# Expert tiles of a large and of a small expert in alternation, with single buffers for each kind

## The reference

```python
def swiglu(xb, wg, wu, wd):
    return (jax.nn.silu(xb @ wg) * (xb @ wu)) @ wd

# hier_moe, cut: 4 groups of 8 experts, top 2, D_MODEL 1024, D_EXPERT 512
def expert_block(args):
    xb, e = args
    return swiglu(xb, lp['w_eg'][e], lp['w_eu'][e], lp['w_ed'][e])
yb = lax.map(expert_block, (xin, block_e)).reshape(n_rows, d)
return jax.ops.segment_sum(yb[dest] * sw[:, None].astype(h.dtype), st, num_segments=t)
```

## Time and profile before

| | us |
|---|---|
| median of 3 runs | 2587.0 |
| lowest and highest | 2582.14 and 2589.04 |
| the profiled execution | 2590.32 |
| span of its instructions | 2589.0 |

### The profile page before, as it was taken

One profiled execution on the slowest core, in us unless ns is written; L12 is line 12 of the kernel. 1 busy time (PEld: TensorE's weight loads), 2 busy tenths in 40 slices (PEclk: granted clock), 3 DMA queues, 4 the chain that ended last, 5 costly groups with the idle time before them and its releaser, 6 DMA issues.

```text
span 2589.0 us, 31253 instructions
## 1 busy us (share of the span) xinstructions
PE 2462.0 (95%) x12362; PEld 1884.7 (73%) x12362; DVE 1414.8 (55%) x2034; ACT 1044.5 (40%) x1570; POOL 288.6 (11%) x256
## 2 busy tenths in 40 slices
PE   6999999999999989888999889999999999999999
PEld 4867768687777766655666577888888777788887
DVE  3575776778547665544445655434444577543442
ACT  2424343343445345554445554223243446422221
POOL 0010211112223201111111010000013000100000
PEclk9999999999999979999999989999999999999999
DMA  7324243432445269999999923232232111323322
GB/s 267 110 73 163 78 162 111 142 97 97 165 160 195 72 233 377 375 381 369 381 386 386 373 99 114 75 112 93 74 125 76 48 50 49 106 83 97 106 78 77
DMA packets 143400, 428.18 MB, mean 165 GB/s; under 512 B 19394, under 2 KB 33986, under 8 KB 142096
## 3 DMA queue, kind: packets, MB, share of 16 engines
q1 hardware_dynamic: 119136, 377.43, 41.1%
q10 hardware_dynamic: 12960, 25.19, 2.7%
q0 software_dynamic: 11152, 23.49, 2.6%
HBM read 411.62 MB, written 31.72 MB: 171 GB/s over the span
## 4 chain that ended last, share of the span: by engine, by line
PE 76%; DVE 9%; DMA 8%; ACT 4%; issue 2%; POOL 1%; SPq 0%; ACTq 0%; POOLq 0%; DVEq 0%
PE bank L666 18%; PE bank L667 18%; PE bank L668 18%; DMA more<-in_ed 4%; DVE HLB L326 3%; PE bank L1216 2%; PE bank L1218 2%; PE bank L1217 2%; DMA raw<-in_ed 2%; PE bank L1273 2%; ACT HLB L315 2%; PE bank L1573 1%; PE bank L1234 1%; PE bank L953 1%; PE bank L1596 1%
## 5 line engine op out<-in xcount | busy, mean ns | idle before, releaser
L326 DVE TENSOR_TENSOR HLB<-raw,HLB 128x1024 fp32r<-128x1024 f32 (+1 forms) x374 | 454.1, 1220 | 475.3 <-ACT HLB L315 471.0
L666 PE MATMUL bank<-HTh,HLB 128*128 128x512 f32 (+1 forms) x1358 | 548.5, 404 | 12.3 <-DVE HLB L326 7.5
L315 ACT ACTIVATE HLB<-raw 128x1024 fp32r<-128x1024 f32 x382 | 381.5, 1007 | 386.9 <-PE bank L668 277.6
L667 PE MATMUL bank<-HTl,HLB 128*128 128x512 f32 (+1 forms) x1358 | 534.0, 393 | 0.0
L668 PE MATMUL bank<-HTh,HLB 128*128 128x512 f32 (+1 forms) x1358 | 533.4, 393 | 0.0
L666 PEld LDWEIGHTS bank<-HTh,HLB 128*128 128x128 f32 x1358 | 257.4, 190 | 99.1 <-issue 27.3
L668 PEld LDWEIGHTS bank<-HTh,HLB 128*128 128x128 f32 x1358 | 257.6, 190 | 59.7
L667 PEld LDWEIGHTS bank<-HTl,HLB 128*128 128x128 f32 x1358 | 257.8, 190 | 56.7 <-issue 1.9
L326 DVE TENSOR_TENSOR HLB<-more,HLB 128x1024 fp32r<-128x1024 f32 x116 | 139.8, 1223 | 71.6 <-ACT HLB L315 68.5
L315 ACT ACTIVATE HLB<-more 128x1024 fp32r<-128x1024 f32 x116 | 121.7, 1062 | 79.3 <-DMA more<-in_ed 66.8
L666 PE MATMUL bank<-FAh,HLB 128*128 128x512 f32 x352 | 139.1, 395 | 0.0
(11 more groups left out here) (601 smaller groups left out, 4256.6 us busy)
## 6 DMA issues: line engine op xcount, KB each, us to landing
raw<-in_f SPq DMA_DIRECT2D x120, 512.0 KB
more<-in_eg SPq DMA_DIRECT2D x77, 512.0 KB
more<-in_ed SPq DMA_DIRECT2D x73, 512.0 KB
raw<-in_eu SPq DMA_DIRECT2D x65, 512.0 KB
more<-in_eu SPq DMA_DIRECT2D x63, 512.0 KB
raw<-in_ed SPq DMA_DIRECT2D x55, 512.0 KB
raw<-in_eg SPq DMA_DIRECT2D x51, 512.0 KB
raw<-in_wada SPq DMA_DIRECT2D x40, 512.0 KB
```

The costliest lines, as they stand in the source:

```text
L315: self.nc.scalar.activation(hi, raw, ACT.Copy).then_inc(*self.w_hi.next(n))
L326: self.nc.vector.tensor_tensor(lo, raw, hi.bitcast(F32), ALU.subtract).then_inc(*self.w_lo.next(n))
L666: mm(bank, ah, bh, start=(start and i == 0), stop=False)
L667: mm(bank, ah, bl, start=False, stop=False)
```

## The change

The diff replaces the list of blocks by two lists: `heavy`, the large experts 0 to 16, and `few`, for each step the small expert that goes with it (none in step 0, 17 to 31 in steps 1 to 15, none in step 16). A step has 12 places m. At places 0 to 7 TensorE takes one gate/up tile of the large expert and then one of the small; at 8 to 11 one down tile of the previous step's large expert and one of its small one. Between places 7 and 8 it turns in the next step's tokens of both; after place 11 it transposes both gated products. In step 16 the down tiles of small expert 31 stand at places 2 to 5. The loads follow the same order.

Each kind has single tiles of its own: `XG`, `XGh`, `XGl`, `YO`, `GT`, `GTh`, `GTl` for the large, `XQ`, `XL`, `GQ`, `GTL`, `YQ` for the small. A new use waits for the end of the former one. The room goes into `more`, which has 6 buffers (`NSLOT`) instead of 5. In this stage splits are planned up to 8 tiles ahead (`AHEAD_MIXED`) instead of 4. GpSimd gathers for step s + 2 once the tokens of step s + 1 are turned in. The part of the output that stays on chip (`kept`) is large expert 16's as before. `in_order` is as before, and so is the number of tiles, matmuls, transposes and splits.

```diff
+NSLOT = 6
+AHEAD_MIXED = 8
+WEAVE = 1
@@ Plan, "lend"
-                self.slots_now = NRAW + NMORE * (len(self.backs) + 1)
-                self.raw_free += [(NRAW + NMORE * len(self.backs) + i, None) for i in range(NMORE)]
+                mixed = len(self.backs) == 1
+                self.ahead = AHEAD_MIXED if mixed else AHEAD
+                lent = range(NRAW + NMORE, NRAW + NMORE + NSLOT) if mixed else range(NRAW, NRAW + NMORE)
+                self.slots_now = lent[-1] + 1
+                self.raw_free += [(i, None) for i in lent]
@@ Plan.advance
-        while self.split < min(len(self.slot), self.at + AHEAD):
+        while self.split < min(len(self.slot), self.at + self.ahead):
@@ pe_experts
+        def few_at(few, s):
+            return 8 if few[s] is not None else 2
...
+            turn_in(heavy[0])
+            for s, b in enumerate(heavy):
+                for m0 in range(0, 12, WEAVE):
+                    for m in range(m0, m0 + WEAVE):
+                        if m < 8:
+                            first(b, "eg" if m < 4 else "eu", m % 4)
+                        elif s:
+                            last(heavy[s - 1], m - 8)
+                    for m in range(m0, m0 + WEAVE):
+                        if few[s] is not None and m < 8:
+                            first_few(few[s], "eg" if m < 4 else "eu", m % 4)
+                        if s and few[s - 1] is not None and 0 <= m - few_at(few, s) < 4:
+                            last_few(few[s - 1], m - few_at(few, s))
+                    if m0 + WEAVE == 8 and s + 1 < len(heavy):
+                        turn_in(heavy[s + 1])
+                        if few[s + 1] is not None:
+                            turn_in_few(few[s + 1])
+                middle(b)
+                if few[s] is not None:
+                    middle_few(few[s])
+            for k in range(4):
+                last(heavy[-1], k)
@@ act_experts
+            def turn_in(s):
+                b = heavy[s]
+                for q in range(2):
+                    act.wait_ge(*S.pe_out.when(("xg", b, q)))
+                    if s:
+                        act.wait_ge(*S.pe_out.when(("eu", heavy[s - 1], 3)))
+                    activation(XGh[:, 4 * q:4 * q + 4, :], ...
@@ pool_experts
+            def gather(s):
+                b = heavy[s]
+                if s:
+                    pool.wait_ge(*S.pe_out.when(("xg", heavy[s - 1], 1)))
...
+            for s in range(len(heavy)):
+                if s + 2 < len(heavy):
+                    gather(s + 2)
+                    if few[s + 2] is not None:
+                        gather_few(s + 2)
+                if s and few[s - 1] is not None and few[s] is None:
+                    scatter_few(few[s - 1])
+                if s:
+                    scatter(heavy[s - 1])
+                if s and few[s - 1] is not None and few[s] is not None:
+                    scatter_few(few[s - 1])
@@ the order
-        blocks = list(range(STATIC))
-        for n in range(LIGHT):
-            blocks += [HEAVY + n, STATIC + n]
+        heavy = list(range(HEAVY))
+        few = [None] + list(range(HEAVY, 32)) + [None]
```

More of the change, by code:

```diff
@@ L500, in build @@
         phase(W1)
[L501 to L512, removed]
+        XG = here("XG", [128, 1024])
+        XQ = here("XQ", [128, 512])
+        XGh = here("XGh", [128, 8, 128], FR)
+        XGl = here("XGl", [128, 8, 128], FR)
+        YO = here("YO", [128, 1024])
         XL = here("XL", [128, 4, 128])
-        phase(W1 + 7680)
+        GQ = here("GQ", [128, 256])
         GTL = here("GTL", [128, 2, 128])
+        YQ = here("YQ", [128, 512])
         phase(W1)
         YI = here("YI", [128, 4, 2, 1024])
-        assert cur[0] == EARLY_YI
+        GT = here("GT", [128, 512])
+        GTh = here("GTh", [128, 4, 128], FR)
+        GTl = here("GTl", [128, 4, 128], FR)
+        more = here("more", [128, NSLOT, 1024])
         phase(W1)
@@ L654, in build @@
                        [raw[:, i, :] for i in range(NRAW)] + [early[:, i, :] for i in range(NMORE)]
-                       + [more[:, i, :] for i in range(NMORE)], HLB, counted.get("tiles", []),
+                       + [more[:, i, :] for i in range(NSLOT)], HLB, counted.get("tiles", []),
                        w_load + w_early + w_more, w_hi, w_lo, pe_out)
@@ L2067, in act_experts, with out_few @@
-            last(len(blocks) - 1)
+                    activation(YO[:, cols(4 * n, 4)], psum[("yo", b, n)][:, :], ACT.Copy, scale=weight).then_inc(
+                        *S.act_out.next(("yo", b, n)))
+            def out_few(s):
+                b = few[s]
+                column = NBLK + b - HEAVY
+                act.wait_ge(*S.pe_out.when(("yo", b, 3)))
+                act.wait_ge(*dve_out.when("wrow"))
+                if few[s - 1] is not None:
+                    act.wait_ge(*S.scattered.when(few[s - 1]))
+                activation(YQ[:, :], psum[("yo", b, 0)][:, :], ACT.Copy, scale=WROW[:, column:column + 1]).then_inc(
+                    *S.act_out.next(("yo", b, 0)))
@@ L2069, in act_combine @@
+            for k in range(4):
+                ring.hi(act, "ed", heavy[-1], k)
+            out(len(heavy) - 1)
         def act_combine():
@@ L2961, in dve_combine @@
+            for k in range(4):
+                ring.lo(dve, "ed", heavy[-1], k)
+            if S.kept:
+                keep(heavy[-1])
         def dve_combine():
@@ L3560, in build @@
                     e.wait_ge(*s.when("experts"))
-                e.wait_ge(*scattered.when(30))
+                e.wait_ge(*scattered.when("all"))
             found = {}
```

518 lines of the change are left out of this document (267 added, 251 removed).

## The result

The kernel after takes 2593.0 us (median of 17 runs, 2589.6 to 2599.2) where the kernel before takes 2584.7 on the same chip (17 runs, 2582.1 to 2590.2). The ratio is 1.0029, 95% interval 1.0022 to 1.0036: slower by 0.3%, where 2564 us and faster were forecast. The profiled execution took 2597.2 us (span 2595.9), 6.9 more than that of before.

The account below looks back on a forecast made before the run. TensorE and the DMA, both nearly full and starving in turns, were taken as the bound. A stage 24.1 us shorter, less 1 us at its end, took the median from 2587.0 to a forecast 2564 us, range 2548 to 2583.

Parts of the forecast that it names:

- the work added: TensorE in the expert stage: 180 round trips of matmul shape against 30, 180 x 0.20 = 36.0 us, ends 25 and 49.
- the pot: TensorE's 50.8 us of idle time in the expert stage, to fall to under 15.
- the sum: Expert stage: TensorE's 524.4 us plus waits and cover, 536.5 us instead of 560.6; 24.1 gained, 23.1 after the end's charge.
- Priced at nothing beyond the sum: Six extra buffers and splits eight tiles ahead: no time of their own; the gated load becomes the sixth instead of fifth.
- the hole: DMA dip at 1186 to 1190 us, where SyncE's load waits for a large tile's buffer; worth 2.1 us.
- shallow queue* rival: Large-tile buffer reuse still gates loads; a third of the hole stays, twice a step: 10 us gained, 2577 us, chance 0.13.
- The price of a round trip: TensorE going from large to small tile shape and back: 0.20 us, between 0.14 and 0.27.
- 488.4: TensorE's us of large tiles, small tiles and transposes in the expert stage, whatever the order.
- shape* rival: Changes of matmul shape on TensorE become the bound at 0.40 us a trip: 2600 us, slower, chance 0.11; break-even 0.33.
- Hidden: SyncE's expert-number reads, four a step instead of two: about 2 us more a step, costing nothing.
- turn-in: Next large expert's tokens, turned in after the eighth pair: hidden by under 1 us; uncovered, 16 to 24 us, chance 0.11.
- The end of the stage: Last scatter, now large expert 15's, and the loads of summed rows waiting for it: charged 1 us, 0 to 3.

Follow-up runs that it names:

- four ahead: The kernel after with splits planned 4 tiles ahead instead of 8 (AHEAD_MIXED = 4), large and small tiles still alternating singly: 2570.9 us, 0.9940 of before.
- by twos: The kernel after with splits planned 4 tiles ahead and two large tiles alternating with two small ones: 2564.3 us, 0.9908 of before.
- the kernel without changes of shape: The kernel after with small experts' matmuls on all 128 columns, half as many: 2583.1 us, 0.9989 of before; with splits 4 ahead, 2566.1 us, 0.9914.

## Why the prediction was wrong

**Right: the work added, and the pot.** TensorE's busy time rose by 36.6 us for a forecast 36.0. With four ahead, alternation one by one gives 0.6% and by twos 0.9%, 15 and 24 us, where the sum had 23.1. That the 24 is so near is no confirmation: by twos has half of the changes of shape for which the sum pays. One by one the stage takes 543.4 us (first to last expert matmul; before 559.6, after 571.6), where the sum had 536.5.

**The step that failed: "Priced at nothing beyond the sum".** Of the six extra buffers and eight tiles ahead I asked how many large tiles the halves cover, and which load is gated at the point of one hole. I did not ask how long the loop from a buffer to the same buffer is, in tiles and in us, for each load of the stage. In the hole the count was right, the fifth load before and the sixth after. But by the planner's order only 4 of a large expert's 12 tiles were reused by the fifth to eighth load before, and the other 8 by the ninth; after, every one is reused by the sixth. With the 8.8 us of a round in the trace of after, six tiles give 1.47 us a tile and 35.2 a step. Against the kernel with four ahead that is 23 us (1.0029 less 0.9940, of 2585 us).

The copy (1.06) and the remainder (1.22) were in the rows; the landing was not, and it is no constant. In the chains of waits from 970 to 1460 us it is 9.1 us on average before, 6.2 after and 9.0 at four ahead; in the kernel before with eight ahead, a load issued when none was on its way landed in 3.7. With the 9.1 of before a step would have come out at 46 us, far too long. So the trace of before could have shown the loop as a danger, but not its price. The *shallow queue* rival named the mechanism and, at 2577, sized it at about half, 13 us given back: it let "a third of the hole stay", a share that no row gave.

**The price of a round trip** was 0.20, with 0.14 and 0.27 as ends, and it is 0.32 by the sum, 0.36 against the kernel without changes of shape. I had discounted the first large matmul's extra 0.08 as owed to the pause ahead of it; an extra of 0.11 comes without a pause too. The Trainium skill, "TensorEngine Tiling (Array Packing)", section "Key Properties", says that changing the tiling mode drains the engine. The trace agrees in that a change has a price; it does not show what the engine does in that time. But 180 x 0.12 = 22 us more of work on TensorE did not come out as 22 us of time: at eight ahead taking all of the changes away returned 10 us, at four ahead 5 to 7, with intervals that overlap. That the busy time rose by just the 36 us is chance: 488.4 + 180 x 0.32 makes 546.0, the 546.5 of the trace, while the 509.9 of before held some 21 us beyond its 488.4, of which its own 30 round trips are some 10 (an estimate, 30 x 0.32) and the rest tails of waits and the lower clock. The *shape* rival gave the right sign and nearly its time (2600), by a cause that the experiments turn down.

**The reads, "Hidden".** They were queued behind the wait for the remainder, and ahead of the load that the loop wants. SyncE waits 47.0 us at L650 (45.7 of it for remainders), 23.6 before (13.3 of it), and taking the extra reads away returned 7 us. I had asked whether SyncE has time, and not whether the read lies in a chain.

**Left out: a bank behind a split.** The prediction went through the single XG, GT and YO and their turn-in, but not through the bank that the small expert's silu frees. It costs some 6 us. The turn-in itself held: TensorE waits for XGh and XGl once each (1.5 and 0.5 us), as it did in the first expert before, and never for a gather.

**The rate.** I used 410 to 412 GB/s from stretches of 2 us for a floor of 507 us. Held over a stage it is 391 to 394. This did not decide the result, but it is the likely reason why by twos and without changes of shape end at the same time.

**The end of the stage** was charged 1 us and returned about 7: from the last expert matmul to the end of the span it is 1095.5 us before (2589.0 - 1493.5) and 1088.1 after. TensorE's matmuls there in order of time, in the kernel before:

```profile
1503.16 1.23 PE L1313 MATMUL bank<-km,YI 128*128 128x128 f32 x4 [4.23 <-DVE YI L2969]
1505.43 2.93 PE L1313 MATMUL bank<-km,YI 128*128 128x128 f32 x12 [1.04 <-DVE YI L2969]
```

These 5.3 us of waits for the summed rows (YI) have no counterpart after, which is most of the 7 us. Why the rows are ready in time was not tried.

The shares of the miss do not add up: the loop took 23 us, and the silu, the reads and the changes of shape are worth 6, 7 and 10 each while the loop is there.

## What to carry to other kernels

Where a buffer's next load waits for the work on the tile in it, work out the loop: copy, remainder, issue and landing, divided by the number of loads until the one that takes the buffer. If this is more than the pace wanted, the loop is the bound, however idle each engine in it looks. Do it for each load, not for the one at a hole, and with a landing time that fits the number of loads on their way, since it grows with them. Planning work further ahead can make that loop shorter in tiles, and so slower: when a buffer is given away is a choice of its own, apart from when its tile is worked on.

## What the runs showed of the hardware

- A round trip between tiles of 128 columns and tiles of 64 costs 0.32 us by the sum of its parts (2.61 for 2.29 us), and 0.36 against the same pairs with all tiles on 128 columns (2.25 us).
- Transfers of 512 KB on one queue held 391 to 394 GB/s over 490 us at best in these kernels, though single stretches of 2 us show 412 and more.
- The time from issue to landing of such a transfer went from 3.7 us with no other on its way to 6.2 on average in after and 9.0 at four ahead.
- The DMA share stood at 1.00 at 371 GB/s (after) and at 1.02 at 391 (four ahead): it hardly tells the two apart.
- After a pause of 3.2 us the granted clock was 0.72 and then 0.50 (1.2 GHz) over the next 4 us, and large matmuls started 0.43 us apart where 0.23 is normal.
- Two reads of a number into a register per step, on the issuing queue, cost the kernel after some 7 us in all, where they lie in the loop that sets the pace, and nothing that could be measured in the kernel by twos at four ahead.
